# Strassen stages of a two-layer trunk: another order of operand sums, weight sums, refills and raw-weight releases

## The reference, cut to what matters

```python
def swiglu(h, w_gate_up, w_down):
    gu = h @ w_gate_up                    # 1024 -> 2 x 2816
    return (jax.nn.silu(gu[..., :D_FF]) * gu[..., D_FF:]) @ w_down   # 2816 -> 1024

for layer in range(DEPTH):                # 0: 1040 tokens, 1: 1024 tokens
    ...
    h = h + swiglu(rms_norm(h, ffn_norm_g[layer]), ffn_w_gate_up[layer], ffn_w_down[layer])
    if layer == N_A_LAYERS - 1:
        k_sh, v_sh = shared_kv(h, kv_norm_g, w_kv)
```

## Time and profile before

| | us |
|---|---|
| median of 3 runs | 2903.98 (2898.47 to 2909.09) |
| the profiled execution | 2907.49 |
| its span in the trace | 2905.7 |
| TensorE busy | 2789.6 (96%) |
| VectorE busy | 1972.0 (68%) |
| GpSimd busy | 1254.1 (43%) |
| ScalarE busy | 1100.9 (38%) |
| mean granted TensorE clock | 0.984 of full |

### The profile page before, as it was taken

The page is one execution under the profiler, slowest core; times in us unless marked ns, Lnnn a source line. Parts: engine busy times, 40 slices in busy tenths (PEclk is TensorE's granted clock), DMA queues, the critical chain, the costliest instruction groups (busy, mean ns, idle before and its releaser), DMA issues. The chain is left out here.

```text
span 2905.7 us, 48520 instructions
## 1 busy us (share of the span) xinstructions
PE 2789.6 (96%) x19378; PEld 2527.1 (87%) x19378; DVE 1972.0 (68%) x2514; ACT 1100.9 (38%) x1968; POOL 1254.1 (43%) x1072
## 2 busy tenths in 40 slices
PE   8999989999989999999998999899999999999998
PEld 7999978888989999999998998788887788887776
DVE  6767536777456777777777444477747888888776
ACT  4211235555443323333434201466734333334333
POOL 2000135665254556555663100233333766664664
PEclk9999989999999999999999999999999999999999
DMA  4333411221202332234431425554310233234432
GB/s 127 90 95 95 119 54 60 73 71 48 70 19 72 109 110 81 99 134 149 147 122 44 147 98 171 144 119 108 82 59 29 95 109 105 87 106 174 155 127 87
DMA packets 214235, 289.82 MB, mean 100 GB/s; under 512 B 9435, under 2 KB 150892, under 8 KB 214012
## 3 DMA queue, kind: packets, MB, share of 16 engines
q1 hardware_dynamic: 203434, 248.42, 27.5%
q0 software_dynamic: 10368, 38.21, 3.9%
q10 hardware_dynamic: 210, 0.07, 0.0%
HBM read 203.56 MB, written 83.12 MB: 99 GB/s over the span
## 5 line engine op out<-in xcount | busy, mean ns | idle before, releaser
L2023 DVE TENSOR_TENSOR RL<-RAW,RH 128x512 fp32r<-128x512 f32 (+1 forms) x408 | 398.0, 976 | 255.1 <-ACT RH L1452 253.4
L1452 ACT ACTIVATE RH<-RAW 128x512 fp32r<-128x512 f32 (+1 forms) x408 | 247.8, 617 | 712.9 <-POOL RAW L1079 271.1
L2680 PE MATMUL PS<-QP,RH 128*128 128x512 f32 x1584 | 497.1, 395 | 0.0
L2683 PE MATMUL PS<-QP,RH 128*128 128x260 f32 x1584 | 417.2, 284 | 0.0
L2682 PE MATMUL PS<-QP,RH 128*128 128x260 f32 x1584 | 416.9, 284 | 0.0
L2680 PEld LDWEIGHTS PS<-QP,RH 128*128 128x128 f32 x1584 | 300.6, 190 | 67.8
L2680 PE MATMUL PS<-QP,RL 128*128 128x512 f32 x792 | 314.7, 397 | 19.0 <-DVE QP L2084 11.7
L2682 PEld LDWEIGHTS PS<-QP,RH 128*128 128x128 f32 x1584 | 302.2, 191 | 0.0
L2683 PEld LDWEIGHTS PS<-QP,RH 128*128 128x128 f32 x1584 | 301.5, 190 | 0.0
L1079 POOL TENSOR_TENSOR RAW<-RAW 128x512 f32<-128x512 f32 (+1 forms) x136 | 206.2, 1517 | 157.0 <-DVE RL L2023 151.7
L2682 PE MATMUL PS<-QP,RL 128*128 128x260 f32 x792 | 226.8, 286 | 26.4 <-DVE RL L2023 11.8
(11 more groups left out here) (361 smaller groups left out, 7102.8 us busy)
## 6 DMA issues: line engine op xcount, KB each, us to landing
RAW<-in_ffn_w_gate_up SPq DMA_DIRECT2D x44, 1024.0 KB, 5.1
s_in<-obuf POOLq DMA_DIRECT2D x32, 520.0 KB, 4.4
raw<-in_gdn_w_in SPq DMA_DIRECT2D x32, 512.0 KB, 4.1
RAW<-in_ffn_w_down SPq DMA_DIRECT2D x16, 1024.0 KB, 5.4
QF<-s_a SPq DMA_DIRECT2D x12, 1040.0 KB, 8.6
QF<-s_a SPq DMA_DIRECT2D x12, 1024.0 KB, 8.2
s_a<-ua SPq DMA_DIRECT2D x22, 520.0 KB, 2.8
s_a<-ua SPq DMA_DIRECT2D x22, 512.0 KB, 3.2
```

The lines of the kernel that those rows point to most:

```text
L1452: act.activation(m.RH[n % m.ring][:, 0:kn, :], m.weight_block(p, i), ACT.Copy).then_inc(m.f_hi[0], 1)
L2023: dve.tensor_tensor(m.RL[n % m.ring][:, 0:kn, :], m.weight_block(p, i), m.RH[n % m.ring][:, 0:kn, :].bitcast(F32), ALU.subtract).then_inc( ...
L2680: done = pe.matmul(acc, w, x, start=first, stop=last)
L2683: done = pe.matmul(acc[:, 1, :], w, x[:, 1, :], start=first, stop=last)
```

## The change

No instruction is added or taken away; the order and some waits are different.

1. **Step order.** In the first two pairs of a chunk products 5 and 6 are swapped: 6, 5. `LAST_STEP` becomes `RAW_DONE`, which leaves product 5 out, since its weights stand in `TS` and not in `RAW`: the slot is released earlier. Because of that GpSimd gets a wait before the sum for i = 5: the low half of (p - 2, 5) must have been read out of `TS`.
2. **Refills.** The first operand of a chunk is refilled before n0 - 3 instead of n0 - 2, and operand 6 before operand 5; loads, high and low parts all go by `REFILL_ORDER`.
3. **Weight sums.** In the third pair of a chunk the sum for i = 1 is issued five steps ahead instead of three; for pair 2 the sums 5 and 3 are issued at a later number.
4. **Mill head.** GpSimd makes the sum (1,6) after the wide subtraction instead of before; ScalarE makes high half 3 ahead of the four full sums; VectorE does the four `gained_less` for `QF5` before low half 3, and `whole_low(4)` after the eviction of step 3.
5. **Key head.** Gain and low half of key weights 6 and 7 are made two or three steps earlier on VectorE, their high halves on ScalarE, and TensorE waits for fewer evictions before the first two chunks of columns.

```diff
-    STEPS += [(p, i) for i in range(5) for p in (_p, _p + 1)] + [(p, i) for p in (_p, _p + 1) for i in (5, 6)]
+    STEPS += [(p, i) for i in range(5) for p in (_p, _p + 1)] + [(p, i) for p in (_p, _p + 1) for i in (6, 5)]
...
-LAST_STEP = [max(STEP_NO[p, i] for i in range(7)) for p in range(NP)]
+RAW_DONE = [max(STEP_NO[p, i] for i in range(7) if i != 5) for p in range(NP)]
+REFILL_ORDER = [0, 1, 2, 3, 4, 6, 5]
...
-    for _i, _back in (((5, 6), (3, 6), (1, 4), (6, -1)), ((5, 3), (3, 3), (1, 2), (6, -1)), ((5, 5), (3, 5), (1, 3), (6, 1)),
-                      ((5, 6), (3, 6), (1, 4), (6, 2)))[_turn]:
+    for _i, _back in (((5, 6), (3, 6), (1, 4), (6, -1)), ((5, 3), (3, 3), (1, 2), (6, -1)), ((5, 5), (3, 5), (1, 5), (6, 1)),
+                      ((5, 4), (3, 4), (1, 4), (6, 2)) if _p == 2 else ((5, 6), (3, 6), (1, 4), (6, 2)))[_turn]:
...
-REFILL_AT = {STEP_NO[GP + 4 * c, 0] + (-2, -1, 1, 2, 4, 5, 7)[i]: (c, i) for c in range(len(DOWN_K)) for i in range(7)}
+REFILL_AT = {STEP_NO[GP + 4 * c, 0] + (-3, -1, 1, 2, 4, 5, 7)[o]: (c, i) for c in range(len(DOWN_K)) for o, i in enumerate(REFILL_ORDER)}
...
-                sp.wait_ge(*since(m.f_lo, LAST_STEP[p - 2] + 1))
+                sp.wait_ge(*since(m.f_lo, RAW_DONE[p - 2] + 1))
...
                     if i == 5:
                         pool.wait_ge(*since(m.f_raw[p % 2], 16 * (p // 2 + 1)))
+                        if p > 1:
+                            pool.wait_ge(*since(m.f_lo, step_done(p - 2, 5)))
...
                 weight_sum(0, 6)
-                weight_sum(1, 6)
                 pool.wait_ge(*since(m.q_g, 8))
                 pool.wait_ge(*since(m.q_t, 4))
                 pool.tensor_tensor(m.q_full(2, 0, 4), m.q_full(2, 0, 4), m.q_full(4, 0, 4), ALU.subtract).then_inc(m.q_p[0], 1)
+                weight_sum(1, 6)
...
                         if l == 7:
+                            block_high(3)
                             act.wait_ge(mm_chunk, ph.mm0 + ph.mm)
                             for k in range(4):
                                 gained(m.q_full(2, k, 1), k, 0, m.q_g)
...
-                        block_high(l - 4)
+                        if l < 7:
+                            block_high(l - 4)
...
                     gained_low(l // 4, l % 4, l, 0, m.q_a, l + 1)
+                    if l == 7:
+                        dve.wait_ge(*since(m.q_t, 4))
+                        for k in range(4):
+                            gained_less(5, k, 4 + k, 0, 4)
                     if l >= 4:
                         block_low(l - 4)
...
-                    if n == 2:
-                        dve.wait_ge(*since(m.q_t, 4))
-                        for k in range(4):
-                            gained_less(5, k, 4 + k, 0, 4)
+                    evict(n - 1)
+                    if n == 4:
                         dve.wait_ge(*since(m.q_p, 5))
                         dve.wait_ge(*since(m.q_t, 8))
                         whole_low(4, m.q_b, 4)
-                    evict(n - 1)
...
+                    if m.layer == 0 and n == len(STEPS) - 3:
+                        gain(6, KVN, 16 * (P_KV.slot0[0] + 1))
+                    if m.layer == 0 and n == len(STEPS) - 2:
+                        lo(6, P_KV.job0 + 1)
...
-                    if m.layer == 0 and n == len(STEPS) - 1:
-                        gain(6, KVN, 16 * (P_KV.slot0[0] + 1))
...
-                lo(6, P_KV.job0 + 1)
+                gain(7, KVN, 16 * (P_KV.slot0[1] + 1))
                 stream_low(7)
+                lo(7, P_KV.job0 + 2)
                 stream_low(6)
-                gain(7, KVN, 16 * (P_KV.slot0[1] + 1))
-                lo(7, P_KV.job0 + 2)
...
-                    if l < 2:
-                        pe.wait_ge(*since(mills[0].f_d, READ_OUT[len(STEPS) - 2 + l]))
+                    if l == 1:
+                        pe.wait_ge(*since(mills[0].f_d, READ_OUT[len(STEPS) - 1]))
                     if l == 0:
                         for ch, (t0, n) in enumerate(ph.chunks):
+                            pe.wait_ge(*since(mills[0].f_d, READ_OUT[len(STEPS) - (2 if ch == 2 else 3)]))
```

More of the change, by code:

```diff
@@ L811, in loads @@
                     if chunk is not None:
-                        for i in range(2, 7):
+                        for i in REFILL_ORDER[2:]:
                             refill(m, chunk, i)
@@ L2082, in refill_low @@
                     kn = DOWN_K[c][1]
-                    dve.wait_ge(*since(m.d_hi, 7 * c + i + 1))
+                    dve.wait_ge(*since(m.d_hi, 7 * c + REFILL_ORDER.index(i) + 1))
                     dve.tensor_tensor(m.q_low(X_OF[i], 0, kn), m.q_full(X_OF[i], 0, kn), m.q_high(X_OF[i], 0, kn).bitcast(F32),
@@ L2669, in product @@
                         c, i = operand_of_step(n)
-                        pe.wait_ge(*since(m.d_lo, 7 * c + i + 1))
+                        pe.wait_ge(*since(m.d_lo, 7 * c + REFILL_ORDER.index(i) + 1))
                     for k in range(kn):
```

4 lines of the change are left out of this document (2 added, 2 removed).

## The result

The changed kernel takes 2881.73 us (median of 4 runs, 2879.63 to 2882.50); the kernel before took 2906.53 beside it. The ratio is 0.9919, interval 0.9906 to 0.9932, so 19.8 to 27.3 us faster. Forecast were 2883.9 us and a gain of 20.05; the span in the trace went from 2905.7 to 2880.7, by 25.0 (without rounding 25.06).

A forecast was written before the change was run, and what follows sets the result against it. TensorE, busy 2789.6 of 2905.7 us, bounds the kernel, so only its idle and lower-clock time can change. Terms 4.5 + 0.85 + 9.8 + 0 + 3.3 + 0 + 1.1 + 0.5 = 20.05 off 2904.0 give 2883.9 us; range 2864 to 2895.

The forecast's parts named there:

- rival A: Heads really open, VectorE and GpSimd meet less, chunk heads gain too: 38 us gain, 2866; chance 0.27.
- B: Only the part heads gain; both mill heads come out even, keys wait for tiles: about 10 us, 2894; chance 0.15.
- C: Slower: moved refill delays low half 155 and eviction 151 at six chunk heads; 11.4 slower, 2915; chance 0.08.
- Mill 0 head: First mill, steps 0 to 8: new stall before step 3, step 4 at 867.15 instead of 871.66; gain 4.5 us.
- Step 19: First mill: earlier load of raw pair 2 shortens the 6.0 us wait; gain 0.85, between 0 and 3.4.
- Part heads: First mill, steps 169, 197, 224, 225: earlier load and sum remove waits and two half-clock stretches; gain 9.8, lower bound 5.
- Chunk heads: Steps 154 to 158 and their like: wait only moves; gain 0, between -2 and +1.5 per head, both mills.
- the sign that I had named for rival C: More idle time at the chunk heads than 4.5 and 6.8 us (mill 0, 1) would speak for C.
- Key head: First key weight: TensorE starts at 1559.05 instead of 1566.20, then waits for tiles; gain 3.3 us, up to 5.3.
- Mill 1: Second mill: head 0, its step-20 wait 1.1, chunk heads 0, part heads 0.5 us gain.
- Step 20: Second mill: wait of 2.66 us, forecast to gain 1.1 us.

The follow-up runs named there:

- later-subtraction run: Changed kernel with GpSimd's wide subtraction after the sum (1,6) and after low half 5: 2882.28 us, ratio 0.9924 to the kernel before.
- the run with the head undone: Changed kernel with sum (1,6), high half 3, `gained_less` and `whole_low(4)` back in their old places: 2888.64 us, ratio 0.9950 to the kernel before.
- no release: Changed kernel without step swap, early raw release and both refill edits: 2887.10 us, ratio 0.9948 to the kernel before.
- sum number alone: Kernel before with only the third pair's sum for i = 1 issued five steps ahead instead of three: 2897.35 us, ratio 0.9974.
- part-head edits alone: Kernel before with steps 5 and 6 swapped, early raw release and third-pair sum for i = 1 five steps ahead: 2901.12 us, ratio 0.9987.
- with the refill order: Kernel before with step swap, early raw release, earlier third-pair sum, and refill 6 ahead of 5, first refill unmoved: 2894.64 us, ratio 0.9966.
- release alone: Kernel before with the step swap, early raw release and GpSimd's wait, the sum still three steps ahead: 2900.12 us, ratio 0.9989.

## Why the prediction was right

The total came out 3.5 us above the forecast gain by the ratio and 5 by the spans, inside the range, and rival A (2866), B (2894) and C (2915) did not come about. That 2881.73 lies only 2.2 us from 2883.9 is in part luck: the kernel before measured 2906.53 beside it and not the 2904.0 from which I subtracted. The sum also had its errors: the head, step 19 and the keys gave more than forecast, mill 1 less. Point by point:

- **Mill 0 head.** The chain was right to 0.25 us (step 3 at 860.74 for 860.85, step 4 at 866.91 for 867.15), and the later-subtraction run shows its cause: without GpSimd's subtraction beside them the same four operations take 3.80 us. The term was mis-sized by what follows it: step 4 took 5.34 us before, largely at 1.2 GHz, and 2.95 after, so 4.75 became 7.14 at step 5. I had counted the clock at the part heads and left it out here; about 1.2 of it is a difference between executions (step 4 took 4.31 in the run with the head undone).
- **Step 19.** 0.83 where 0.85 was forecast for the wait. In step 19 itself another 0.86 were won at the half clock, but that isn't shown to be the edit's: without the release, with the wait still at 5.95 and 6.06 us, two runs (no release, sum number alone) won 0.97 and 0.73 there, and three with the release and the head of before (part-head edits alone, with the refill order, release alone) between 0.30 and -0.15. That the load came 5.9 us sooner and gave so little was right.
- **Part heads.** 10.57 for 9.8. The amount was right, and so was it that the sum for i = 1 came too late; the account of what had to be moved was not complete: the early release and the early sum each cover the first two waits, so the 1.75 and 2.08 hang on neither alone, and the release needs the refill order, whose price (6.1 us without it) the prediction did not name.
- **Chunk heads.** Forecast 0 and between -2 and +1.5 each; mill 0 gave 0.65 over three. Refill and low half still wait for one another: the wait moved from step 154 (1.1 us) to step 158, which grew from 3.12 to 4.60. In mill 1 the sign that I had named for rival C, more than 6.8 us of idle time at the first head, did appear (7.53), step 184 waited 3.61 instead of 2.19, step 212 2.38 instead of 1.12, and the three heads took 2.3 us back where 0 was forecast. So C had its place right and its size wrong: 2.3 for three heads, not 2.5 at each. That the earlier refill is the cause isn't shown: undoing it gave 1.1 us in mill 1, the run with no refill edit at all lost the same 2.3 at its chunk heads, and the spread between nearly equal code is as large.
- **Key head.** 3.9 for 3.3, and the chain as forecast: TensorE started 1.2 us after the last step (forecast 1.1), its wait for the last `YA` tile ended 13.4 us after it (14.0), the first matmul over squares started 17.7 us after it (18.3, before 21.6; the 1579.60 of the prediction is where it starts, not where it ends). Of the 8.21 us wait half was won, the other half turned into waits of 0.40, 1.54 and 1.72 for tiles and squares. Undoing it gave 4.4.
- **Mill 1.** 0.45 for 1.6. The head gave -1.0 for 0: step 3 waited 3.77 (4.0), but step 4 was 2.8 us late (forecast 1.6). Step 20 gave 2.7 for 1.1: 1.3 of its wait and 1.4 in the step behind it, which the sum left out. The chunk heads took 2.3 us back (0), and the last part head gave 1.1 (0.5).

## What to carry to other kernels

When two engines hold each other up, reordering the short operations changes which of them is held, not for how long (8.17 us for four in both orders). Moving the long operation itself took 4.4 us off the wait before step 3, cutting it in pieces took 0.2; but the move held another operation and delayed whoever needed its result, and the time of the whole kernel stayed the same. So follow the moved operation to its reader. An edit that reorders steps has a partner in each table that feeds them, so test edits in the pairs in which they belong before adding up their gains. A wait of TensorE can be worth more than its length, because of the half-clock stretch behind it: put both into the sum at every wait, not at some, and the stretch as a range, since it differs between executions.
